# A diffusion backbone on one core: the conditioning projection as row sums on VectorE, GpSimd and ScalarE

## The chip, the cores and the metric

One core of one Trainium2 chip runs the whole kernel in one launch. The metric is the device time of that launch in microseconds (us).

## What is computed

Four layers work on 256 latent tokens and 256 context tokens of width 1024, in fp32. Each layer has a token mixer (neighbourhood attention, retention, convolution, attention again) and a gated feed-forward part (FFN). In front of each stands an RMS norm that is shifted and scaled by the conditioning, and behind each the result is gated by it:

```python
silu_c = jax.nn.silu(c); silu_cc = jax.nn.silu(c_ctx)[None, :]
for i in range(DEPTH):
    mx = jnp.split((silu_c @ ada_w[i] + ada_b[i])[:, None, :], 6, axis=-1)
    mc = jnp.split((silu_cc @ ada_w[i] + ada_b[i])[:, None, :], 6, axis=-1)
    hx = modulate_norm(xs, norm_mix[i], mx[0], mx[1])
    ...
    xs = xs + mx[2] * yx
    hx = modulate_norm(xs, norm_ffn[i], mx[3], mx[4])
    xs = xs + mx[5] * conv_ffn(hx, ffn_w_up[i], ffn_w_dw[i], ffn_b_dw[i], ffn_w_down[i])
```

The conditioning projection is a product of two vectors (one for the context, one for the latent tokens) with four matrices `ada_w[i]` of 1024 by 6144: 6144 features per layer, which are 48 chunks of 128 features. A layer's chunks come in the order shift, scale, gate of the mixer, then shift, scale, gate of the FFN, 8 chunks each.

## The kernel before, in words

Activations lie by feature: 128 features on the partitions, 8 chunks of features, 512 tokens along the row (context, then latent). A dense layer is a row of **tiles**, each 128 output features by 512 tokens in one PSUM bank; a tile takes one **group** of weights (128 x 1024, 512 KB; `_tile_groups`) for 1024 inputs. Every fp32 product is made as three products of a high and a low part (`three`, lines 554 to 556): high by high, low activation by high weight, high activation by low weight. So a group is loaded by SP into `raw` (`refill`, line 402), ScalarE copies it to the high part `Whi` (line 1007), VectorE subtracts for the low part `Wlo` (line 1284, `split`), and TensorE runs 8 x 3 matmuls of 512 columns. There are four slots; the engines split a group three tiles ahead (`LEAD`). SP loads a slot again when TensorE has used it (`weights_used`).

Order of the work in layer 0 behind the first norm: 16 tiles of keys and queries (the mix), 8 groups of values with tokens on the partitions (`tokens_major`), 8 pairs of heads (`pair`, 8 units each: scores on TensorE, bias and maximum on VectorE, exponential on ScalarE, transposes, product with the values), 8 tiles of the output projection (`projected`). Then the second norm (`norm_halves`): the last tiles are made context half first, so that the norm of the context half runs beside the latent half. The FFN is 11 **laps** of 4 tiles (up) and 8 tiles of three groups (down: 8, 8 and 6 blocks of 128, that is 22 x 3 matmuls each). In a lap, VectorE makes three taps of a convolution from tiles 0 and 2 (lines 1702, 1704, 1707), and multiplies tiles 1 and 3 with the GELU (1712) and subtracts for a low part (1716). GpSimd sums the squares for the next norm, one tile behind `residual` (lines 452 and 454: a square and a sum, 512 wide), and in layer 0 stages one head's queries at a time in `Qz` (line 503). In the stages with heads, units wait for each other on three engines.

The conditioning, `mod`, is made from `ada_w` in **slices** of 512 features: 12 per layer, 48 in all. The first four are made ahead of everything (`ada_raw`), the other 44 in places between the tiles: 4 in the mix, 2 in the output projection of layer 0 (`ADA_IN_O`), one in each of the 33 up laps of layers 0 to 2, and 3, 1 and 1 in the down stages (`ada_down`). A slice is loaded by SP (`load_ada`, line 394: four DMAs of 512 KB behind a wait for the slice before), and then made by `ada_slice` (8 products of 32 stationary columns with 512 moving ones, line 653), `ada_rows` on VectorE (line 1295: copy to SBUF), `ada_cols` (4 transposes, line 667), and `ada_store` (lines 1304 and 1306: a small sum, and an add of the bias). TensorE also waits for `mod_ready` ahead of the values (line 739).

Each engine runs its own program in order, and waits on semaphores.

## Time and profile before

| | |
|---|---|
| median of 3 runs | 2718.21 us (2706.47 to 2720.6) |
| the profiled execution | 2714.99 us, of it span 2713.2 us |
| TensorE busy | 96% of the span |
| VectorE, ScalarE, GpSimd busy | 55%, 34%, 10% |
| mean granted TensorE clock | 0.985 |
| DMA | 337.36 MB, mean 124 GB/s |

PE is TensorE's matmuls, PEld its weight loads, DVE VectorE, ACT ScalarE, POOL GpSimd, SP SyncE; a name with a q behind it is the engine's queue. `out<-in` are the program's names, then come partitions x elements. In brackets stands how long the engine sat idle before the instruction, and who ended that.

### The profile page before, as it was taken

How to read it: one execution, taken by the hardware profiler on the slowest of the kernel's cores; microseconds unless marked ns; L12 is line 12 of the kernel's file. 1: busy time of each engine (PE TensorE's matmuls, PEld its weight loads, DVE VectorE, ACT ScalarE, POOL GpSimd, SP SyncE). 2: the span in 40 equal slices, each digit the busy share in tenths (PEclk: the TensorE clock that was granted, in tenths of full speed). 3: DMA queues.
4: the chain of work that ended last, by engine and by line, in shares of the span. 5: the costliest groups of instructions: out<-in, count | busy, mean ns of one | idle time of the engine just before them, and what ended most of it. 6: DMA issues, size and time to landing. Idle time of an engine off the chain costs nothing. (4 is left out here: it accounts for less than half of the span.)

```text
span 2713.2 us, 38419 instructions
## 1 busy us (share of the span) xinstructions
PE 2617.0 (96%) x13796; PEld 2115.7 (78%) x13796; DVE 1482.1 (55%) x2247; ACT 914.3 (34%) x1443; POOL 265.6 (10%) x252
## 2 busy tenths in 40 slices
PE   6999999999999999999999998999999999999999
PEld 3667787777788866788777887878777788778999
DVE  4765645554345344426555338877555436856774
ACT  2225623222232123323222226443222213345543
POOL 5100030000110020030000110003000014102000
PEclk8999999999999999999999999989999999999999
DMA  8531035544423321324444331112545434311455
GB/s 271 166 116 36 0 125 186 178 170 161 156 79 108 111 68 47 124 93 140 178 173 159 125 99 57 55 55 98 177 167 178 155 101 122 109 57 55 157 184 179
DMA packets 94877, 337.36 MB, mean 124 GB/s; under 512 B 11840, under 2 KB 13632, under 8 KB 94656
## 3 DMA queue, kind: packets, MB, share of 16 engines
q1 hardware_dynamic: 90176, 324.28, 34.7%
q0 software_dynamic: 2880, 8.92, 1.5%
q10 hardware_dynamic: 1728, 2.85, 0.3%
q8 instruction: 68, 1.11, 0.2%
q14 instruction: 25, 0.20, 0.0%
HBM read 334.95 MB, written 1.05 MB: 124 GB/s over the span
## 5 line engine op out<-in xcount | busy, mean ns | idle before, releaser
L554 PE MATMUL bank<-Hhi,Whi 128*128 128x512 f32 (+1 forms) x2440 | 883.2, 362 | 37.1 <-DVE Hlo L1340 16.1
L555 PE MATMUL bank<-Hlo,Whi 128*128 128x512 f32 (+1 forms) x2440 | 861.5, 353 | 0.0
L556 PE MATMUL bank<-Hhi,Wlo 128*128 128x512 f32 (+1 forms) x2440 | 860.2, 353 | 0.0
L1284 DVE TENSOR_TENSOR Wlo<-raw,Whi 128x1024 fp32r<-128x1024 f32 x424 | 526.7, 1243 | 387.2 <-ACT Whi L1007 385.4
L1007 ACT ACTIVATE Whi<-raw 128x1024 fp32r<-128x1024 f32 x424 | 447.5, 1057 | 855.9 <-DMA raw<-in_weights 855.4
L554 PEld LDWEIGHTS bank<-Hhi,Whi 128*128 128x128 f32 x2440 | 464.6, 190 | 139.0 <-issue 60.8
L555 PEld LDWEIGHTS bank<-Hlo,Whi 128*128 128x128 f32 x2440 | 465.0, 191 | 63.6 <-issue 4.6
L556 PEld LDWEIGHTS bank<-Hhi,Wlo 128*128 128x128 f32 x2440 | 464.7, 190 | 63.1
L554 PE MATMUL bank<-Ghi,Whi 128*128 128x512 f32 (+1 forms) x770 | 268.6, 349 | 0.0
L556 PE MATMUL bank<-Ghi,Wlo 128*128 128x512 f32 (+1 forms) x770 | 267.1, 347 | 0.0
L555 PE MATMUL bank<-Glo,Whi 128*128 128x512 f32 (+1 forms) x770 | 266.2, 346 | 0.0
L452 POOL TENSOR_TENSOR square<-X 128x512 f32<-128x512 f32 (+1 forms) x58 | 92.0, 1587 | 1517.8 <-DVE X L1399 1509.3
L1702 DVE TENSOR_SCALAR hb<-bank,fff 128x512 f32<-128x512 f32 (+1 forms) x88 | 65.4, 743 | 250.2 <-PE bank L556 248.4
L554 PEld LDWEIGHTS bank<-Ghi,Whi 128*128 128x128 f32 x770 | 144.6, 188 | 22.7 <-DVE X L1399 4.2
L1245 ACT ACTIVATE hb<-hb 128x512 f32<-128x512 f32 (+1 forms) x88 | 51.0, 580 | 327.6 <-DVE hb L1707 327.6
L555 PEld LDWEIGHTS bank<-Glo,Whi 128*128 128x128 f32 x770 | 144.5, 188 | 19.4
L556 PEld LDWEIGHTS bank<-Ghi,Wlo 128*128 128x128 f32 x770 | 144.6, 188 | 18.9
L1399 DVE SCALAR_TENSOR_TENSOR X<-bank,mod,X 128x256 f32<-128x256 f32 x84 | 37.4, 479 | 151.6 <-PE bank L556 151.6
L560 PE MATMUL bank<-Whi,Hhi 128*128 128x512 f32 x256 | 101.8, 398 | 8.0 <-DVE mod L1306 5.4
L1712 DVE TENSOR_TENSOR hb<-hb,bank 128x512 f32<-128x512 f32 (+1 forms) x88 | 54.4, 619 | 86.7 <-PE bank L556 86.7
L561 PE MATMUL bank<-Whi,Hlo 128*128 128x512 f32 x256 | 101.3, 396 | 0.0
L562 PE MATMUL bank<-Wlo,Hhi 128*128 128x512 f32 x256 | 101.0, 395 | 0.0
(194 smaller groups left out, 2879.2 us busy)
## 6 DMA issues: line engine op xcount, KB each, us to landing
raw<-in_weights SPq DMA_DIRECT2D x424, 512.0 KB, 3.3
ada_ring<-in_ada SPq DMA_DIRECT2D x176, 512.0 KB, 5.6
ada_raw<-in_ada SPq DMA_DIRECT2D x16, 512.0 KB, 15.8
rel_in<-in_rpb POOLq DMA_DIRECT2D x48, 128.0 KB, 4.5
decay_t<-in_dist POOLq DMA_DIRECT2D x4, 640.0 KB, 4.2
X<-in_x ACTq DMA_DIRECT2D x1, 2048.0 KB, 10.0
out_y<-X SPq DMA_DIRECT2D x1, 1024.0 KB, 4.8
cos_sin<-in_rope ACTq DMA_DIRECT2D x1, 256.0 KB, 14.2
```

The source lines that it names most:

```text
L452: g.tensor_tensor(square[:, c % 2, tok], X[:, c, tok], X[:, c, tok], ALU.mult).then_inc(sum_step, 1)
L554: t.matmul(dst, Whi[:, st.slot, w], hi, start=start, stop=False)
L555: t.matmul(dst, Whi[:, st.slot, w], lo, start=False, stop=False)
L556: return t.matmul(dst, Wlo[:, st.slot, w], hi, start=False, stop=stop)
L560: t.matmul(dst, hi, Whi[:, st.slot, w], start=start, stop=False)
L561: t.matmul(dst, lo, Whi[:, st.slot, w], start=False, stop=False)
L562: return t.matmul(dst, hi, Wlo[:, st.slot, w], start=False, stop=stop)
L1007: a.activation(Whi[:, st.slot, :], raw[:, st.slot, :], ACT.Copy).then_inc(hi_split, 1)
L1245: a.activation(cv[:, k, tok], cv[:, k, tok], ACT.Gelu_apprx_tanh).then_inc(gelu_done, 1)
L1284: v.tensor_tensor(Wlo[:, st.slot, :], raw[:, st.slot, :], Whi[:, st.slot, :].bitcast(F32), ALU.subtract)\
L1702: v.tensor_scalar(c3, u3, f[:, 0, 1:2], f[:, 0, 3:4], ALU.mult, ALU.add).then_inc(ffn_tap, 1)
L1712: v.tensor_tensor(cv[:, k, tok], cv[:, k, tok], bank[m][:, tok], ALU.mult)\
```

## The change

The first four slices stay. The other 176 chunks of 128 features are no longer made on TensorE. Their weights lie by feature: a chunk is 128 features on the partitions by 1024 inputs, so that one feature's sum runs along a row. At the start TensorE spreads the two conditioning vectors over all partitions (16 products of 128 columns, in the first stage behind slice 1), and ScalarE copies them to `cond`. Then a chunk is loaded by ScalarE's queue into one of three slots of `cond_w`, 512 KB each.

Of a **shared** chunk (115 of them) VectorE makes the latent sum with one scalar_tensor_tensor over 1024 elements that also sums its row (`weigh`), GpSimd then multiplies the slot in place with the context vector (`scale_weights`), ScalarE copies it onto itself and sums the row (`sum_products`), and VectorE adds the bias three chunks later (`cond_store`). Of the other 61 chunks VectorE makes both sums, one after the other. ScalarE loads the slot again when the chunk is summed (`reload`).

Where the chunks go: 8 shared ones beside the values of layer 0, one per group; 8 shared ones beside the pairs of heads, one per pair; 8 not shared in the output projection, two each behind tiles 0 to 2, one each behind 3 and 4; three shared ones in each of the 33 up laps; in the down stages 23 not shared in layer 0 (two each behind groups 0 and 1, one each behind 2 to 20), and 15 in layers 1 and 2 each (groups 0 to 18, but not 3, 7, 11, 15). The loop over pairs of layer 0 is written out on VectorE, ScalarE and GpSimd, as is the first up lap on VectorE. The rope tables are now loaded at the start of the retention instead of at the start of the kernel. The bytes loaded are the same.

```diff
-ADA_SLICES = 6 * D // 512
+MODS = 6 * D // P
 ADA_FIRST = 4
 QUAD = P // 4
-ADA_IN_O = {0: 8, 2: 9}
+COND_SLOTS = 3
+PER_LAP = 3
+IN_V = 8
+IN_HEADS = 8
+IN_O = (0, 0, 1, 1, 2, 2, 3, 4)
+IN_DOWN = ((0, 0, 1, 1) + tuple(range(2, 21)), tuple(g for g in range(20) if g % 4 != 3))
 HALVED = (0, 2, 1, 1, 1, 2, 1, 0)
...
+        p["hosts"] = layer < DEPTH - 1
+        if p["hosts"]:
+            p["cond_up"] = cond + (IN_V + IN_HEADS + len(IN_O) if layer == 0 else 0)
+            p["cond_down"] = p["cond_up"] + PER_LAP * FC // 2
+            cond = p["cond_down"] + len(IN_DOWN[layer > 0])
+            p["cond_end"] = cond
...
+        _, cond_w = region(("cond_skip", [P, 2 * FC * T], F32), ("cond_w", [P, COND_SLOTS, GROUP], F32))
+        _, cond = region(("cond_in_skip", [P, RETENTION], F32), ("cond", [P, 2, D], F32))
+        _, cos_sin = region(("cos_skip", [P, 2 * C * T + 2 * TB * D], F32), ("cos_sin", [P, 2, SEQ], F32))
...
+        def shared(n):
+            return n < IN_V + IN_HEADS or any(p["hosts"] and p["cond_up"] <= n < p["cond_down"] for p in layers)
+        def shared_before(n):
+            return sum(shared(q) for q in range(n))
+        def weighed(n):
+            return 2 * (n + 1) - shared_before(n + 1)
...
-            load_ada(ADA_FIRST)
             for layer, p in enumerate(layers):
-                if layer == 0:
-                    refill(p["mix"], 4, (1,), ADA_FIRST + 1)
-                    refill(p["v"], 2)
-                    refill(p["o"], 1, (0, 2), ADA_FIRST + 5)
-                    refill(p["o"] + SLOTS, 1)
...
+            def scale_weights(n, per=0, i=0):
+                pool.wait_ge(cond_weighed, weighed(n) + per * i)
+                w = cond_w[:, n % COND_SLOTS, :]
+                g.tensor_tensor(w, w, cond[:, 0, :], ALU.mult).then_inc(cond_scaled, 1)
...
+                if layer == 0:
+                    pool.wait_ge(cond_ready, 2)
+                    pool.wait_ge(qz_cleared, 2)
+                    for n in range(IN_V):
+                        scale_weights(n)
...
+                    if layer == 0:
+                        pool.wait_ge(cond_scaled, IN_V + i)
...
+                        pool.wait_ge(q_staged, 2 * i + 2)
+                        scale_weights(IN_V + i)
...
+                if p["hosts"]:
+                    with pool.Fori(0, FC // 2) as i:
+                        for q in range(PER_LAP):
+                            scale_weights(p["cond_up"] + q, PER_LAP, i)
...
-                        if p["ada"] and m == 1:
-                            ada_slice(p["ada"], 1, i)
-                        if p["ada"] and m == 2:
-                            ada_cols(p["ada"] + i)
...
+                if s == 1:
+                    for r in range(2):
+                        for k in range(C):
+                            last = t.matmul(bank[2 * r + k // 4][:, P * (k % 4):P * (k % 4 + 1)],
+                                            csilu[:, k, r:r + 1].to_broadcast([P, P]), ident[:, :],
+                                            start=True, stop=True)
+                        last.then_inc(cond_spread, 1)
...
+            def load_weights(n, per=0, i=0):
+                act.dma_start(cond_w[:, n % COND_SLOTS, :], ada[4 * ADA_FIRST + n + per * i, :, :])\
+                    .then_inc(cond_loaded[n % COND_SLOTS], 16)
+            def sum_products(n, per=0, i=0):
+                nth = shared_before(n)
+                act.wait_ge(cond_scaled, nth + 1 + per * i)
+                w = cond_w[:, n % COND_SLOTS, :]
+                a.activation(w, w, ACT.Copy, accum_out=cond_sum[:, n % COND_SLOTS, 0:1]).then_inc(cond_summed, 1)
+            def reload(n, end, per=0, i=0):
+                if n + COND_SLOTS < end:
+                    if shared(n):
+                        act.wait_ge(cond_summed, shared_before(n) + 1 + per * i)
+                    else:
+                        act.wait_ge(cond_weighed, weighed(n) + per * i)
+                    load_weights(n + COND_SLOTS, per, i)
...
+                        if layer == 0 and s == 5:
+                            sum_products(IN_V + i)
+                            reload(IN_V + i, p["cond_end"])
...
+                act.wait_ge(weights_used, p["mix"])
+                act.dma_start(cos_sin[:, :, :], rope).then_inc(cos_loaded, 16)
...
+                        if p["hosts"] and m >= 2:
+                            for q in ((0,) if m == 2 else (1, 2)):
+                                sum_products(p["cond_up"] + q, PER_LAP, i)
+                                reload(p["cond_up"] + q, p["cond_end"], PER_LAP, i)
...
+                    for n in in_down(layer, m - 1):
+                        reload(n, p["cond_end"])
...
+            for r in range(2):
+                act.wait_ge(cond_spread, r + 1)
+                for k in range(2):
+                    last = a.activation(cond[:, r, 512 * k:512 * (k + 1)], bank[2 * r + k][:, :], ACT.Copy)
+                last.then_inc(cond_ready, 1)
...
+            def weigh(n, spare, per=0, i=0, follows=True):
+                slot = n % COND_SLOTS
+                dve.wait_ge(cond_loaded[slot], 16 * (n // COND_SLOTS + 1) + 16 * (per // COND_SLOTS) * i)
+                if follows:
+                    cond_store(n - COND_SLOTS, per, i)
+                    dve.wait_ge(mod_ready, 4 * ADA_FIRST + n - COND_SLOTS + 1 + per * i)
+                w = cond_w[:, slot, :]
+                first = weighed(n - 1) if n else 0
+                for q, r in enumerate((1,) if shared(n) else (0, 1)):
+                    if first + q:
+                        dve.wait_ge(cond_weighed, first + q + per * i)
+                    last = v.scalar_tensor_tensor(spare[:, :, :].rearrange("p k t -> p (k t)"), w, 1.0, cond[:, r, :],
+                                                  ALU.mult, ALU.mult, accum_out=cond_sum[:, slot, r:r + 1])
+                    last.then_inc(cond_weighed, 1)
+            def cond_store(n, per=0, i=0):
+                slot, k = n % COND_SLOTS, 4 * ADA_FIRST + n
+                earlier = 2 * MODS if k + per >= 2 * MODS else 0
+                dve.wait_ge(cond_weighed, weighed(n) + per * i)
+                if shared(n):
+                    dve.wait_ge(cond_summed, shared_before(n) + 1 + per * i)
+                v.tensor_tensor(mod_slices[:, bass.ds(k - earlier + per * i, 1), :], cond_sum[:, slot:slot + 1, :],
+                                bias_slices[:, bass.ds(k + per * i, 1)].unsqueeze(2).to_broadcast([P, 1, 2]), ALU.add)\
+                    .then_inc(mod_ready, 1)
+            def cond_flush(end):
+                for n in range(end - COND_SLOTS, end):
+                    cond_store(n)
+            def ada_store(index):
...
+                dve.wait_ge(mod_ready, MODS * layer + (6 if part else 3) * C)
                 whole = C - (HALVED[r] if r < 2 * DEPTH else 0)
                 for m in range(whole):
                     st = Step(first + stride * m)
                     for q in range(stride - 1):
                         split(st.ahead(q))
+                        for n in hosted(stride * m + q):
+                            weigh(n, hb)
                     dve.wait_ge(weights_used, st.ahead(stride - 1).n + 1)
                     residual(layer, part, bank[m % 4], m, tok)
                     split(st.ahead(stride - 1))
-                    if m in slices:
-                        ada_rows(slices[m])
-                    if m - 1 in slices:
-                        ada_store(slices[m - 1], earlier)
+                    for n in hosted(stride * m + stride - 1):
+                        weigh(n, hb)
+                if end:
+                    cond_flush(end)
                 if whole < C:
                     for q in range(stride * (C - whole) - 2):
                         split(Step(first + stride * whole + q))
                     norm_halves(r, tuple(range(whole, C)), add_half(layer, part),
                                 [Step(first + stride * C - 2 + n) for n in range(2)])
-            def tokens_major(first, count, dst):
...
+                            if hosts:
+                                weigh(4 * y + quarter, hb, follows=4 * y + quarter >= COND_SLOTS)
...
+                        if layer == 0 and s == 0:
+                            weigh(IN_V + i, hb)
...
+                        if p["hosts"] and m < PER_LAP:
+                            weigh(p["cond_up"] + m, square, PER_LAP, i, not first)
+                projected(layer, 1, p["down"], 3, tok, lambda g: in_down(layer, g))
+                if p["hosts"]:
+                    cond_flush(p["cond_end"])
```

## Rows read from the trace of the kernel before

**Rows 1.** The page, busy time of each engine, share of the span and instructions.
```profile
PE 2617.0 (96%) x13796; PEld 2115.7 (78%) x13796; DVE 1482.1 (55%) x2247; ACT 914.3 (34%) x1443; POOL 265.6 (10%) x252
```

**Rows 2.** The view of waits, TensorE's: engine, line, releaser, us in total, times, longest.
```profile
PE bank L554 <- DVE Wlo L1284: 13.6, 5, 6.2
...
PE bank L667 <- DVE rows L1295: 12.5, 4, 6.4
PE bank L560 <- DVE mod L1306: 5.4, 1, 5.4
```

**Rows 3.** Timeline of TensorE, an up lap of layer 0: start us, us, engine, line, operation.
```profile
470.29 0.39 PE L556 MATMUL bank<-Hhi,Wlo 128*128 128x512 f32 x1
...
475.73 0.39 PE L556 MATMUL bank<-Hhi,Wlo 128*128 128x512 f32 x1
...
480.49 0.39 PE L556 MATMUL bank<-Hhi,Wlo 128*128 128x512 f32 x1
...
482.66 0.50 PE L554 MATMUL bank<-Hhi,Whi 128*128 128x512 f32 x1
...
488.05 0.39 PE L556 MATMUL bank<-Hhi,Wlo 128*128 128x512 f32 x1
...
488.63 0.47 PE L554 MATMUL bank<-Hhi,Whi 128*128 128x512 f32 x1
```

**Rows 4.** Timeline of VectorE: the copy of a slice's rows, in two laps.
```profile
483.25 0.68 DVE L1295 COPY rows<-bank 128x512 f32<-128x512 f32 x1
...
507.60 0.68 DVE L1295 COPY rows<-bank 128x512 f32<-128x512 f32 x1
```

**Rows 5.** Timeline of VectorE: the same lap, tiles 0 and 1.
```profile
475.80 0.81 DVE L1702 TENSOR_SCALAR hb<-bank,fff 128x512 f32<-128x512 f32 x1 [3.34 <-PE bank L556]
...
478.31 1.22 DVE L1284 TENSOR_TENSOR Wlo<-raw,Whi 128x1024 fp32r<-128x1024 f32 x1
480.91 0.69 DVE L1712 TENSOR_TENSOR hb<-hb,bank 128x512 f32<-128x512 f32 x1 [1.38 <-PE bank L556]
481.52 1.22 DVE L1284 TENSOR_TENSOR Wlo<-raw,Whi 128x1024 fp32r<-128x1024 f32 x1
```

**Rows 6.** Timelines of GpSimd and of VectorE near 53 us.
```profile
52.92 6.74 POOL L488 TENSOR_TENSOR rel<-rel_in,mask 128x3072 f32<-128x3072 f32 x1 [8.11 <-DMA rel_in<-in_rpb]
...
53.26 6.69 DVE L1340 SCALAR_TENSOR_TENSOR Hlo<-hb,mod,Hhi 128x256 fp32r<-128x256 f32 x1 [0.19 <-ACT Hhi L1037]
```

**Rows 7.** Timeline of GpSimd near the start: one square, one sum, 512 wide.
```profile
13.32 1.03 POOL L452 TENSOR_TENSOR square<-X 128x512 f32<-128x512 f32 x1
14.44 1.26 POOL L454 TENSOR_TENSOR total<-total,square 128x512 f32<-128x512 f32 x1
```

**Rows 8.** VectorE's groups by form: busy us, mean ns, then idle before.
```profile
L1572 DVE SCALAR_TENSOR_TENSOR hb<-OT,gn,hb 128x512 f32<-128x512 f32 x8 | 6.0, 751 | 26.9 <-ACT hb L1172 26.9
...
L1590 DVE SCALAR_TENSOR_TENSOR Wc<-bank,cvb,odd 128x512 f32<-128x512 f32 x8 | 6.0, 745 | 0.1
```

**Rows 9.** ScalarE's groups by form: the copy of a group, the read of the accumulator.
```profile
L1007 ACT ACTIVATE Whi<-raw 128x1024 fp32r<-128x1024 f32 x424 | 447.5, 1057 | 855.9 <-DMA raw<-in_weights 855.4
...
L1111 ACT ACTIVATION_READ_ACCUMULATOR prob<-bank,peak 128x1 f32 x96 | 19.0, 198 | 0.0
```

**Rows 10.** Timelines near 223 us, VectorE and TensorE, and of a pair of heads.
```profile
223.43 2.48 DVE L1430 COPY V<-bank 128x512 f32<-128x512 f32 x4
...
223.01 1.02 PE L755 MATMUL bank<-QK,Qz 128*128 128x256 f32 x4
...
258.52 0.16 DVE L1485 RECIPROCAL rinv<-psum_p 128x1 f32<-128x1 f32 x1 [0.83 <-PE bank L773]
...
259.57 0.43 DVE L1477 TENSOR_TENSOR bank<-bank,rel 128x256 f32<-128x256 f32 x1 [0.46 <-PE bank L755]
```

**Rows 11.** Timeline of VectorE at the second norm.
```profile
383.21 0.48 DVE L1391 SCALAR_TENSOR_TENSOR X<-bank,mod,X 128x256 f32<-128x256 f32 x1 [2.40 <-PE bank L556]
```

**Rows 12.** Timeline of TensorE in the first stage: four transposes of 128 columns.
```profile
22.18 0.66 PE L667 MATMUL bank<-ident,rows 128*128 128x128 f32 x4
```

More of the change, by code:

```diff
@@ L91, in plan @@
 def plan():
-    group, tile, ready = 0, 0, 0
+    group, tile, ready, cond = 0, 0, 0, 0
     layers = []
@@ L387, in _, with refill @@
                 sp.dma_start(raw[:, s, :], weights[s, :, :]).then_inc(raw_loaded[s], 16)
-            def load_ada(first, per=0, i=0):
-                if not (per == 0 and first == ADA_FIRST):
-                    sp.wait_ge(ada_used, first - ADA_FIRST + per * i)
-                for q in range(4):
-                    sp.dma_start(ada_ring[:, q, :], ada[4 * first + q + 4 * per * i, :, :]).then_inc(ada_loaded[q], 16)
-            def refill(first, laps, ada_after=(), ada_first=0):
+            def refill(first, laps):
                 with sp.Fori(0, laps) as i:
@@ L1238, in ffn @@
                 a.preload_act_table(ACT.Gelu_apprx_tanh)
+                if layer and p["hosts"]:
+                    for n in range(COND_SLOTS):
+                        load_weights(p["cond_up"] + n)
                 for i in bodies(act, FC // 2):
@@ L1400, in residual, with projected @@
                 last.then_inc(tile_free, 1)
-            def projected(layer, part, first, stride, tok, slices, earlier):
+            def projected(layer, part, first, stride, tok, hosted, end=0):
                 r = 2 * layer + 1 + part
+                dve.wait_ge(mod_ready, MODS * layer + (6 if part else 3) * C)
                 whole = C - (HALVED[r] if r < 2 * DEPTH else 0)
@@ L1421, in projected, with tokens_major @@
                                 [Step(first + stride * C - 2 + n) for n in range(2)])
[L1423 removed]
+            def tokens_major(first, count, dst, hosts=False):
                 for i in bodies(dve, count // 2):
@@ L1685, in ffn @@
                 s0 = 1 if last_layer else 0
-                for i in bodies(dve, FC // 2):
+                for i, first in peeled(dve, FC // 2):
                     for m in range(4):
```

140 lines of the change are left out of this document (58 added, 82 removed).

## The prediction

> **What bounds the kernel now.** I read the engines' busy shares first: TensorE is busy in 96% of the span, VectorE in 55%, ScalarE in 34%, GpSimd in 10% [rows 1]. So time on TensorE is worth its full length, if the others can take the work. TensorE's waits came next: little is left in them, and part of it is the conditioning's own: 12.5 us behind the copy of a slice's rows, 5.4 us for `mod` ahead of the values [rows 2]. Then the timeline of one up lap, since 33 of the 44 slices lie in laps. A tile without a slice takes 475.73 - 470.29 = 5.44 us, 24 matmuls at 0.227 us [rows 3]. A lap takes 507.60 - 483.25 = 24.35 us [rows 4]. Four tiles are 21.76 us, so a slice costs TensorE **2.59 us**: one sees 2.17 us between two matmuls where the products stand, 0.58 us where the transposes stand [rows 3], the rest in slower matmuls behind them.
>
> **What is removed.** 44 slices x 2.59 = 114 us of TensorE. Of the 17.9 us of waits I take 10 back: the longest (6.4 us) falls in the first tiles of the mix, where VectorE is late anyway and TensorE would meet the next wait. Saved: 124 us. This is the profiled execution's account (2715.0 us, 3 us below the median shown).
>
> **The price of a chunk.** VectorE: 256 elements take 0.48 us [rows 11], 512 take 0.75 us [rows 8], so 1024 take 1.29 us. Neighbours overlap by 0.09 us (a split is 1.22 us long, 1.13 from start to start), which leaves 1.21. The trace shows no sum along with such an instruction. Its read of the accumulator is bounded by nothing and by ScalarE's 0.20 us [rows 9]; I take 0.15, nearer to the row. With the store (0.15) and a wait on itself (0.12) a shared chunk is 1.63 us, one that VectorE sums twice 3.11 us (another 0.12 between the sums). GpSimd: 512 elements take 1.26 us [rows 7], 3072 take 6.74 us [rows 6], so 1024 take 2.35 us. ScalarE: a copy of 1024 (1.06 us), its read (0.20 us [rows 9]) and the issue of a DMA (0.4), about 1.7 us; at 34% busy this is hidden outside the heads. The 176 loads are the old bytes, moved from SP's queue to ScalarE's; SP's weights no longer queue behind four loads of a slice, which I count as nothing. Its rope load costs VectorE one landing at the start of the retention, 1 us at most on TensorE.
>
> One more price is in the rows: while GpSimd ran its 6.74 us sum, VectorE's instruction with two SBUF operands, 0.48 us elsewhere, took 6.69 us and ended with it [rows 6]. The two exclude each other. `Wlo`, `Glo`, `weigh` and the store have two SBUF operands; the taps and the multiply by a bank have not.
>
> **Up laps.** VectorE: an even tile 478.31 - 475.80 + 1.13 = 3.64, an odd one (481.52 - 480.91) + 1.13 + 0.61 = 2.35 (`Glo` has the width of the multiply) [rows 5]; twice both 12.0, with queue time 12.3 us. Three shared chunks add 4.9. GpSimd's product starts as a chunk's first sum ends. After tile 0 and tile 2 come, on VectorE, a multiply (0.6, no lock) and a split, which waits 1.4 us for GpSimd; after tile 1 come taps, 2.5 us without lock, which cover its 2.35. So 12.3 + 4.9 + 2.9 = **20.1 us in a lap of 21.76**: hidden, with 1.7 us to spare. Splits run three tiles ahead, about 6.5 us early. If that cover went, each microsecond above 21.76 would cost 33.
>
> **Output projection of layer 0.** VectorE per tile: residual 0.8, split 1.14, and GpSimd's square and sum for the norm (1.03 + 1.26 [rows 7]) that now meet a busy VectorE: 4.2 us. Two chunks add 6.2 behind tiles 0 to 2, one adds 3.1 behind 3 and 4: 3 x 10.4 + 2 x 7.3 + 4.2 + 0.5 of stores = 50.5 us, from the end of tile 0 at 5.4 us. VectorE is free for the norm at 56, where today it adds the second context half (as at 383.21 [rows 11]) some 38 us after the stage's start. All of what follows on TensorE hangs on that norm: **+17 us**. Bounds: 10 if GpSimd's work fits into gaps, 22 with loads late.
>
> **Down stages.** Layer 0, a group of 4.99 us (22 x 0.68 / 3): split 1.14, a third of the residual 0.27, chunk 3.11, a third of GpSimd's 2.25: 5.2 with the waits (`weigh` stands in all of 21 groups, twice in two). 21 x 0.25 + 2 x 3.1 = **+12 us** at the norm behind it; bounds 3 and 18. Layers 1 and 2: 15 chunks in 21 groups, 7 x (3.4 + 0.8 + 2.25) + 15 x 3.1 = 92 of 105 us: hidden.
>
> **Values and heads.** The queries of head 0 are now staged in `Qz` behind GpSimd's eighth product, which waits for the last `weigh`: 223.43 (VectorE's last split is done there, the copies of V start [rows 10]) + 1.6 + 2.35 + 0.1 + 0.6 = 228.1, against scores at 223.0 [rows 10]: **+5**. In a pair VectorE gets 1.63 us and ScalarE 1.7 us into a ring without much play; VectorE's idle moments just ahead of the next long unit are 0.83 and 0.46 us [rows 10]. I take 1.2 us per pair, **+10**; bounds 0 and 8 x 3.3 = 27.
>
> **Start.** 16 products of 128 columns behind slice 1; four transposes of that width take 0.66 us [rows 12], so at least 2.6 us, at most three times that in full fp32. Data is waited for there in part: **+3**, bounds 0 and 8.
>
> **Sum.** 2715 - 124 + 17 + 12 + 5 + 10 + 3 + 1 = **2639 us**, 2.9% below the median of before.
>
> **A rule against this change.** With no sum along the row, two fp32 SBUF operands cost nothing: 751 ns with both in SBUF, 745 ns with one in PSUM [rows 8]. The Trainium skill (Vector Engine (DVE) Microarchitecture Reference, Points that are easy to get wrong) says that such a scalar_tensor_tensor with two SBUF sources that are not bf16 runs at half rate, as no port is left for the accumulator. By the rows above this isn't so; none of them has an accumulator, so it is rival 1.
>
> **Rival 1, slower: the summing instruction takes two passes.** Then 1024 elements take 0.2 + 2 x 1.08 = 2.3 us, 1.1 more per sum. A lap becomes 20.1 + 3.3 = 23.4 us on VectorE, above 21.76, which is where it begins to decide: with the slack of the splits spent, about +48 us over 33 laps. The down group of layer 0 becomes 7.4 us (+57), those of layers 1 and 2 overrun by 27 each, the output projection by 17, the heads by 9. Together 185: **2824 us**. For it: no row has the sum. Against it: the equal times of rows 8. 9%.
>
> **Rival 2: no overlap of GpSimd and VectorE at all.** Each product is pushed into VectorE's path, by a lock asked for at the wrong moments or a product in place that is slower than the sum of rows 7: 17.2 + 7.05 = 24.3 us per lap, +2.5 x 33 = 83, of which the lead of the splits takes back some 15. **2707 us**, with a tail above. For it: rows 6. Against it: taps and waits for TensorE leave 9 us of a lap unlocked. 11%.
>
> **Rival 3: the covers hold everywhere.** Heads, norms and start cost 10 instead of 48: **2600 us**. It needs free time on VectorE at the two norms, which the sums deny. 13%.
>
> **Rival 4: the change doesn't relieve TensorE in full,** because loads from ScalarE's queue come late (a reload stands behind a split and a sum) and `weigh`, and every split behind it, waits: each lap has 10 us between a reload and its use, so only the output projection is exposed: 2655 us, inside the forecast.
>
> **How the numbers follow.** Forecast 65% (rival 4 with it), rival 1 9%, rival 2 11%, rival 3 13%, 2% for what I don't see. The forecast's own bounds: all low terms 2639 - 7 - 9 - 10 - 3 - 2 = 2608, all high 2639 + 5 + 6 + 17 + 5 + 8 = 2680. The range 2600 to 2706 takes in rival 3 and the edge of rival 2. A change under 0.5% (13.6 us) can't be told from none here. Faster: forecast, rival 3 and a third of rival 2, 0.82. Same: 0.06. Slower: rival 1, the tail of rival 2, 0.12.
>
> **What would show it.** Right: no products of slices but the first four's; up laps of 21.8 us in all three layers; the scalar_tensor_tensor with a sum at 1.3 us, GpSimd's product at 2.3 to 2.5 us; splits of 2.5 us next to ones of 1.2 us; VectorE's residual rows without idle time in the first two projections, and TensorE waiting for `Hlo` behind both norms of layer 0; VectorE near 1800 us busy. Wrong: laps longer than 22.5 us, or `Wlo` as the main wait of TensorE there; sums above 2 us (rival 1); ScalarE's `prob` late in the heads by far more than 1.2 us per pair.

## The result, and the profile after

The kernel after takes 2620.3 us, median of 4 runs (2613.0 to 2621.1), against 2717.4 us before in the same job. The ratio is **0.965, 95% interval 0.962 to 0.967**: 3.5% faster. The forecast was 2639 us, 2.9% faster, with a range of 2600 to 2706.

The page of the kernel after, busy time of each engine, answers to [rows 1]:

```profile
PE 2521.8 (96%) x12948; PEld 2093.5 (80%) x12948; DVE 1887.9 (72%) x2765; ACT 1044.2 (40%) x1677; POOL 557.3 (21%) x367
```

TensorE has lost 95 us of busy time and is still busy in 96% of the span: what was taken from it shortened the kernel almost one for one. VectorE got 406 us more, GpSimd 292, ScalarE 130. Its waits (engine, line, releaser, us in total, times, longest), against [rows 2]:

```profile
PE bank L575 <- DVE Wlo L1339: 20.2, 11, 6.2
...
PE bank L688 <- POOL total L455: 6.6, 2, 5.9
...
PE bank L762 <- DVE V L1517: 5.9, 2, 4.9
```

The waits for `rows` and `mod` are gone. Those for `Wlo` are not the chunks' doing (19.2 us in experiment 1, which has none). Two stand out in their place, once each: TensorE waits 5.9 us for GpSimd's last sum ahead of the second norm, and 4.9 us ahead of the first scores. The view puts the second down to VectorE's copies of V, but GpSimd stages head 0's queries just as late, and experiment 9 shows that this was the wait that ended last (the scores start at 208.03 us):

```profile
207.32 1.27 POOL L517 COPY Qz<-QK 64x512 f32<-64x512 f32 x2
```

An up lap of layer 0, VectorE's timeline (start us, us, engine, line), against [rows 4, 5]:

```profile
505.14 0.81 DVE L1789 TENSOR_SCALAR hb<-bank,fff 128x512 f32<-128x512 f32 x1 [1.55 <-PE bank L577]
...
508.79 0.15 DVE L1374 TENSOR_TENSOR mod<-cond_sum,bias_ada 128x2 f32 x1
509.07 1.22 DVE L1363 SCALAR_TENSOR_TENSOR square<-cond_w,cond 128x1024 f32<-128x1024 f32 x1
510.22 0.08 DVE L1363 DVE_READ_ACCUMULATOR square<-cond_w,cond 128x1 f32 x1
510.25 0.69 DVE L1799 TENSOR_TENSOR hb<-hb,bank 128x512 f32<-128x512 f32 x1
510.86 3.01 DVE L1339 TENSOR_TENSOR Wlo<-raw,Whi 128x1024 fp32r<-128x1024 f32 x1
...
526.90 0.81 DVE L1789 TENSOR_SCALAR hb<-bank,fff 128x512 f32<-128x512 f32 x1 [1.53 <-PE bank L577]
```

and GpSimd's product in it:

```profile
510.38 2.40 POOL L461 TENSOR_TENSOR cond_w<-cond_w,cond 128x1024 f32<-128x1024 f32 x1 [8.48 <-DVE square L1363]
```

The lap takes 526.90 - 505.14 = **21.76 us**, four tiles of 5.44. VectorE has one idle moment of size in it, 1.55 us, ended by TensorE (the others are of about 0.15 us): it keeps up. A sum of 1024 takes 1.22 us and its accumulator read 0.08. The split that starts at 510.86, while GpSimd multiplies (510.38 to 512.78), takes 3.01 us, not 1.22.

The output projection, VectorE and GpSimd:

```profile
329.93 0.88 DVE L1481 SCALAR_TENSOR_TENSOR X<-bank,mod,X 128x256 f32<-128x256 f32 x2 [6.30 <-PE bank L577]
...
331.85 1.00 DVE L1374 TENSOR_TENSOR mod<-cond_sum,bias_ada 128x2 f32<-128x2 f32 x1
...
334.15 2.20 DVE L1363 SCALAR_TENSOR_TENSOR hb<-cond_w,cond 128x1024 f32<-128x1024 f32 x1
...
338.89 0.87 DVE L1481 SCALAR_TENSOR_TENSOR X<-bank,mod,X 128x256 f32<-128x256 f32 x2
```

```profile
330.88 1.95 POOL L453 TENSOR_TENSOR square<-X 128x512 f32<-128x512 f32 x1 [24.98 <-DVE X L1481]
332.91 2.36 POOL L455 TENSOR_TENSOR total<-total,square 128x512 f32<-128x512 f32 x1
```

A tile with two chunks takes VectorE 8.96 us against TensorE's 5.44. Both sides pay for each other: the square takes 1.95 us and the sum 2.36, against 1.03 and 1.26 alone [rows 7], and on VectorE a store of 0.15 us takes 1.00 and a sum 2.20. The square's 1.95 us aren't the chunks' doing: in experiment 1, which has none, it takes as long beside the split, and the sum 1.29.

### The profile page after: what moved, and what is told of

The parts are those of the page before. It is cut to its first block and busy times, and to the rows that moved or that the text cites. A ratio compares the mean times of both kernels' runs of the same rounds, so it can differ in the third digit from the quotient of the medians.

```text
span 2618.7 us, 37653 instructions
## 1 busy us (share of the span) xinstructions
PE 2521.8 (96%) x12948; PEld 2093.5 (80%) x12948; DVE 1887.9 (72%) x2765; ACT 1044.2 (40%) x1677; POOL 557.3 (21%) x367
## 5 line engine op out<-in xcount | busy, mean ns | idle before, releaser
L1339 DVE TENSOR_TENSOR Wlo<-raw,Whi 128x1024 fp32r<-128x1024 f32 x424 | 638.6, 1508 | 243.1 <-ACT Whi L1009 241.1
L461 POOL TENSOR_TENSOR cond_w<-cond_w,cond 128x1024 f32<-128x1024 f32 x115 | 276.8, 2407 | 559.3 <-DVE square L1363 516.6
L453 POOL TENSOR_TENSOR square<-X 128x512 f32<-128x512 f32 (+1 forms) x58 | 84.8, 1463 | 689.0 <-DVE X L1481 680.1
L1363 DVE SCALAR_TENSOR_TENSOR hb<-cond_w,cond 128x1024 f32<-128x1024 f32 x138 | 185.8, 1346 | 4.7
L577 PEld LDWEIGHTS bank<-Ghi,Wlo 128*128 128x128 f32 x770 | 144.4, 188 | 21.2
L1026 ACT ACTIVATE cond_w<-cond_w 128x1024 f32<-128x1024 f32 x115 | 121.0, 1052 | 36.2 <-POOL cond_w L461 35.6
L1363 DVE SCALAR_TENSOR_TENSOR square<-cond_w,cond 128x1024 f32<-128x1024 f32 x99 | 121.2, 1224 | 11.7
```

The source lines that it names most:

```text
L453: g.tensor_tensor(square[:, c % 2, tok], X[:, c, tok], X[:, c, tok], ALU.mult).then_inc(sum_step, 1)
L461: g.tensor_tensor(w, w, cond[:, 0, :], ALU.mult).then_inc(cond_scaled, 1)
L577: return t.matmul(dst, Wlo[:, st.slot, w], hi, start=False, stop=stop)
L1026: a.activation(w, w, ACT.Copy, accum_out=cond_sum[:, n % COND_SLOTS, 0:1]).then_inc(cond_summed, 1)
L1339: v.tensor_tensor(Wlo[:, st.slot, :], raw[:, st.slot, :], Whi[:, st.slot, :].bitcast(F32), ALU.subtract)\
L1363: last = v.scalar_tensor_tensor(spare[:, :, :].rearrange("p k t -> p (k t)"), w, 1.0, cond[:, r, :], ALU.mult, ALU.mult, accum_out=cond_su ...
```

## The experiments

I compare stages by waypoints in the profiled executions. "Values" is from the first product of V to the first scores, "heads" from there to the first transposes of O, "projection" from the first matmul of the output projection to the reciprocal of the latent half's root in the norm behind it, "FFN" from that reciprocal to the same one a norm later. The stretch ahead of the values, from the first matmul of the mix, is left out: in kernels whose work there is the same it takes from 109.1 us (experiment 11) to 117.6 (experiment 1), with 113.8 in the kernel after, and why isn't known. Such a difference is part of the total times, so the price of a single edit is better read from its stage. Medians are of 4 to 12 runs, those of before of 4 to 17. All times in us:

| kernel | time | ratio to before | values | heads | projection | FFN of layer 0 |
|---|---|---|---|---|---|---|
| before | 2717.4 | 1 | 45.3 | 110.1 | 58.3 | 404.7 |
| before, no slices | 2592.3 | 0.955 (0.951 to 0.958) | 43.9 | 110.0 | 53.2 | 368.2 |
| before, unrolled | 2713.3 | 0.999 (0.998 to 1.001) | 45.2 | 109.0 | 59.9 | 406.5 |
| after | 2620.3 | 0.965 (0.962 to 0.967) | 49.1 | 109.4 | 68.9 | 369.6 |
| after, no chunks | 2600.8 | 0.958 (0.955 to 0.962) | 44.0 | 109.0 | 53.1 | 369.6 |
| after, no squares | 2602.6 | 0.958 (0.956 to 0.960) | 49.1 | 108.6 | 54.8 | 369.6 |

**1. What the new work costs: all chunks left out.** `mod` is 0 behind the first four slices.

```diff
 def weigh(n, spare, per=0, i=0, follows=True):      # also scale_weights, sum_products, load_weights, reload, cond_store
-    ...
+    pass
+dve.wait_ge(mod_ready, 16); dve.sem_inc(mod_ready, 176)
```

> The kernel after, with all 176 chunks left out (loads, sums, products, stores; the entries of mod behind the first four slices are 0 and marked as ready at the start). Theory, from the waypoints of the kernel after: the new work costs about 4 us ahead of the heads, 0 to 1 in them, 10.6 in the output projection, 1 in the first down stage and nothing in laps, some 17 us in all: about 2602 us, the laps 21.76 us as with the chunks, the first projection's end 10 us earlier. Rival: the heads' sums cost what I predicted (10 us) and the unrolled loops of pairs hide it: then the stretch of the heads gets about 10 us shorter and the time is near 2592. Second rival: the loads of the chunks or the busier engines slow the laps or the gate and output stages of the retention: below 2590.

Measured 2600.8 us (2598.9 to 2601.7): all 176 chunks cost **19.5 us** (the three stages below sum to 21.2; the profiled execution's stretch ahead of the values was 3.8 us longer here). The table says where: values 5.1, heads 0.4, projection 15.7, and nothing in the FFN, where 56 of them lie. The row that closes the projection is VectorE's reciprocal, at 392.53 us in the kernel after and here at

```profile
374.25 0.17 DVE L1359 RECIPROCAL token_root<-token_root 128x4 f32<-128x4 f32 x1
```

**2. What the slices cost: before without its 44.** `ada_slice`, `ada_cols`, `ada_rows`, `ada_store` and `load_ada` are taken out behind the first four slices, `mod` is 0 there.

> The kernel before, with its 44 slices behind the first four left out (their loads, products, transposes, copies and stores; mod is 0 there). My account of what is removed was 44 x 2.59 = 114 us of TensorE and 10 us of waits: about 2594 us for a profiled execution at 2715. If a slice's cost in the trace were partly a wait that something else takes over, more than 2605. Rival: every wait for rows and mod goes too, 17.9 us, and the time is 2583.

Measured 2592.3 us (2590.1 to 2596.3), **123.8 below** before's 2716.1 in that job. The 44 x 2.59 us and 10 us of waits hold, to the microsecond and so partly by luck: the interval of the ratio alone is 113 to 133 us, and the profiled executions differ by 118.7. The stage that is least disturbed bears the price of a slice out: the FFN of layer 0 loses 36.5 us with its 14 slices, 2.61 each. The difference of 8.5 us to experiment 1 (3.8 in the profiled executions) is what the rest of the change costs. Of it one sees 0.9 us in the retention, where the rope tables are now loaded, and 1.4 to 1.5 in each FFN of layers 0 to 2. At the start the first reciprocal comes at 35.6 us against 35.0, but in kernels with the same start it comes anywhere from 35.3 to 38.7. The part in the FFNs wasn't foreseen. It shows in all kernels of the new form looked at, with and without chunks, as a step of 0.233 us between matmuls in the down stage of layer 0 (15.40 us per tile) against 0.229 (15.11); which edit causes it stays open.

**3. The lock: up chunks summed twice on VectorE,** so that GpSimd does nothing in the laps.

```diff
 def shared(n):
-    return n < IN_V + IN_HEADS or any(p["hosts"] and p["cond_up"] <= n < p["cond_down"] for p in layers)
+    return n < IN_V + IN_HEADS
```

> The kernel after, with the chunks of the up laps summed twice on VectorE, as those of the down stages are: GpSimd and ScalarE have no part in them. Theory of the lock: VectorE's lap is 12.3 us of its old work and 3 x 2.76 of chunks, 20.6, below 21.76 as with shared chunks (20.2), because the products no longer hold up the splits: every split in a lap 1.22 us long, laps 21.76, the time that of the kernel after within 0.3% (2620). Rival: the splits' 3.01 us have another cause (the weights, the port of PSUM), so they stay, the lap is 12.3 + 2.9 + 8.3 = 23.5 us on VectorE and the time rises by some 50 us to 2670.

Measured 2616.2 us (2615.6 to 2618.3), ratio 0.964 (0.960 to 0.967), the same as after. The split of the same place in the lap, and all splits by VectorE's groups (busy us, mean ns):

```profile
511.93 1.22 DVE L1334 TENSOR_TENSOR Wlo<-raw,Whi 128x1024 fp32r<-128x1024 f32 x1
```

```profile
L1334 DVE TENSOR_TENSOR Wlo<-raw,Whi 128x1024 fp32r<-128x1024 f32 x424 | 533.9, 1261 | 232.7 <-ACT Whi L1005 230.7
```

```profile
L1339 DVE TENSOR_TENSOR Wlo<-raw,Whi 128x1024 fp32r<-128x1024 f32 x424 | 638.6, 1508 | 243.1 <-ACT Whi L1009 241.1
```

The first two are this kernel, the third the kernel after. GpSimd's share of the laps costs VectorE 105 us of blocked splits and saves it 99 sums of 1.27 us, 126 us. VectorE's idle moment in the lap is as long in both kernels, 1.55 and 1.58 us: in the laps, the help of two other engines is worth next to nothing. The Trainium skill (SBUF — State Buffer, Who interferes with whom) says that VectorE and GpSimd share a pair of ports by an exclusive lock, and that the one that issues second is blocked until the first ends; the trace agrees: the split that starts 0.48 us into the product ends 1.09 us behind it, about a full split (1.22 us, 1.13 from start to start) after the product's end.

**4. Where VectorE begins to decide: one more sum per up chunk.**

```diff
+                if per:
+                    v.scalar_tensor_tensor(spare[:, :, :].rearrange("p k t -> p (k t)"), w, 1.0, cond[:, 1, :],
+                                           ALU.mult, ALU.mult, accum_out=extra[:, 0:1]).then_inc(cond_again, 1)
```

> The kernel after, with one more sum of the same form by VectorE for each chunk of the up laps (99 more; it is the price that rival 1 of the prediction had put on a summing instruction, 1.14 us). VectorE has 1.55 us free in a lap and gets 3 x 1.3 = 3.9 us more (with the wait for its accumulator): if VectorE decides from there on, a lap becomes 24.1 us, 2.35 x 33 = 78 us less some 5 per stage for the lead of the splits, so 2620 + 63 to 78 = 2683 to 2698. Rival: part of the sums falls into time in which VectorE would wait for GpSimd's lock anyway, a lap of 22.7 us, 2650.

Measured 2686.3 us (2683.0 to 2689.9), 66 us more than after. TensorE's first wait by size, and two taps of VectorE one lap apart:

```profile
PE bank L577 <- DVE Wlo L1341: 70.5, 85, 6.2
```

```profile
511.46 0.75 DVE L1803 SCALAR_TENSOR_TENSOR hb<-bank,fff,hb 128x510 f32<-128x510 f32 x1 [0.16 <-DVE hb L1800]
...
535.22 0.75 DVE L1803 SCALAR_TENSOR_TENSOR hb<-bank,fff,hb 128x510 f32<-128x510 f32 x1 [0.16 <-DVE hb L1800]
```

A lap is 23.76 us, 2.0 above TensorE's, where 2.35 were expected. So the bound of rival 1 is real: 3.8 us more per lap (3 x 1.27), a little over the 3.3 that two passes per sum would have cost there, takes two thirds of the gain of 97 us away, and by the prediction the down stages would have come on top. That the change pays hangs on the sum running in one pass.

**5. The projection: its chunks without GpSimd's squares.** The norm behind it then sees the last square only.

```diff
+                if r == 1:
+                    pool.sem_inc(sum_step, 2)
+                    return
                 g.tensor_tensor(square[:, c % 2, tok], X[:, c, tok], X[:, c, tok], ALU.mult).then_inc(sum_step, 1)
```

> The kernel after without GpSimd's squares and sums for the second norm (the norm then sees only the last square), which separates the two parts of the 10.6 us that the output projection got longer: the sums themselves, and what GpSimd's locks add to VectorE's instructions there (a second sum of 2.19 us, a store of 1.00 us). Without them VectorE's tile with two chunks should take 8.95 - 1.8 = 7.1 us and one with one chunk less in proportion; the norm comes 7 to 9 us earlier, about 2612. If the locks add nothing and the sums alone fill VectorE, 2618.

Measured 2602.6 us (2599.5 to 2604.2), 10 us further down than expected. VectorE's residual rows of tiles 0 and 1:

```profile
327.28 0.88 DVE L1484 SCALAR_TENSOR_TENSOR X<-bank,mod,X 128x256 f32<-128x256 f32 x2 [7.89 <-PE bank L580]
...
334.42 0.87 DVE L1484 SCALAR_TENSOR_TENSOR X<-bank,mod,X 128x256 f32<-128x256 f32 x2
```

A tile is 7.14 us, as expected, still above 5.44; but the projection is 54.8 us, 14.1 below after and 1.6 above the kernel without chunks. So **14.1 of the 15.7 us come only where the chunks meet GpSimd's squares and sums**, and the eight chunks without them cost 1.6 us or a little more (experiment 1 has the squares, this kernel hasn't). My expectation counted the lock on VectorE's side alone (1.8 us per tile). The 14.1 us have three parts. VectorE's last residual row ahead of the norm starts 48.8 us after the stage's start against 40.4: **8.3 us** of lock. The context half's reciprocal comes 11.4 us later, so **3.1** more: GpSimd is late itself, its last square and sum queue behind those of the tile before and end at 376.04 us, 2.8 after VectorE's residual rows, and TensorE waits 5.9 us for them (up to 0.9 of the 3.1 are already the clock: from its first matmul behind the wait to the reciprocal it takes 2.3 us, in experiment 1 1.4). From that reciprocal to the latent half's it takes 14.2 us against 11.5: **2.7** more, for TensorE's granted clock is at its lower level, 1.2 GHz, behind the wait. Windows (us, busy of each engine, then clock, DMA share, GB/s) of the kernel after and of this one:

```profile
377.00:382.00 5.00, 5.00 (x23) 4.83 (x23) 1.09 (x3) 0.26 (x1) 1.23 (x2) 0.50 0.10 40
```

```profile
361.50:366.50 5.00, 5.00 (x43) 4.95 (x42) 2.90 (x8) 1.17 (x3) 0.00 (x0) 1.00 0.32 107
```

TensorE makes 23 matmuls in 5 us there instead of 43.

**6. Squares on ScalarE,** for the first six tiles of X; the sums stay on GpSimd, and nothing is left out.

```diff
+                def square_early(c):
+                    act.wait_ge(tile_free, FREE0 + p["mix_tile"] + 24 + 1 + c)
+                    act.wait_ge(sum_step, sum_first(1) + 1 + 2 * max(0, c - 1))
+                    a.activation(square[:, c % 2, :], X[:, c, :], ACT.Square).then_inc(squared, 1)
```

> The kernel after, with the squares of the first six chunks of X for the second norm made by ScalarE (busy 28% of that stage) and only their sums left to GpSimd. In the run without GpSimd's squares and sums the output projection and the norm took 14.1 us less (54.8 against 68.9 us from the first matmul of the stage to the image's reciprocal), but that kernel left work out. Theory: GpSimd's two instructions per tile and VectorE's exclude each other, and what is late in the end is GpSimd's last total: with one of the two gone, 7 to 12 of the 14.1 us come back, 2609 to 2613. Rival: the sums (1.26 us) are the half that hurts, or ScalarE's squares put its splits back: under 4 us, 2617 or more.

Measured 2614.9 us (2612.1 to 2615.7), ratio 0.962 (0.960 to 0.964): 5.5 us better, and the projection 63.3 us, 5.5 less. Less than expected, more than the rival said. Of the 5.5 us, 0.8 are the clock: TensorE still waits 4.6 us and still falls to the lower level (0.50), but comes back sooner. A tile takes VectorE 8.1 us, since the sum alone still blocks a `weigh`, and is blocked itself, 2.24 us for 1.26:

```profile
350.50 2.24 POOL L456 TENSOR_TENSOR total<-total,square 128x512 f32<-128x512 f32 x1 [5.86 <-ACT square L1175]
```

**7. The projection's chunks in the heads,** as shared ones, two per pair (`IN_HEADS = 16`, `IN_O = ()`, `weigh` at units 0 and 4).

> The kernel after, with the 8 chunks of the output projection of layer 0 moved into the heads as shared chunks (two per pair, at units 0 and 4). Theory: the output projection gets its old length back (-10.6 us at the norm behind it, VectorE done with the residuals before TensorE's last tiles), and the heads have room for a second sum of 1.3 us on VectorE and of 1.7 us on ScalarE in a pair of 13.16 us (VectorE 75% busy there, ScalarE 74%): 0 to 3 us more, so 2620 - 9 = 2611. Rival: each sum in the ring costs about 1.2 us, as I had predicted for the first: +10 in the heads, 2620.

Measured 2609.4 us (2606.3 to 2611.2), ratio 0.961 (0.959 to 0.962): 11 us better than after. The projection is back at 53.2 us; the heads take 114.9 us, 5.5 more. The first sum of a pair was nearly free (0.4 us for eight), the second costs 0.7 us each.

**8. Was the heads' cost hidden by the unrolled loops?**

```diff
-                with dve.Fori(1, C) as i:
-                    pair(i, False)
+                for i in range(1, C):
+                    pair(i, False)
```

The same for ScalarE and GpSimd, layer 0 only.

> The kernel before, with the loops over the pairs of layer 0 unrolled on GpSimd, ScalarE and VectorE as the change has them. If the unrolled loops hide a cost of the heads' sums, the heads get about 10 us shorter here, 2708. If they do nothing and the sums stand in idle time, the time is that of before, 2717, and the stretch of the heads about as long as before (110.1 us from the first scores to the first transposes).

Measured 2713.3 us, ratio 0.999 (0.998 to 1.001). The heads take 109.0 us against 110.1: the unrolling gives 1.1 us, no more. The sums stand in idle time, which the kernel after shows too. A sum in a pair, and TensorE in the same microseconds, with no idle time noted in front of any of its rows:

```profile
222.74 1.23 DVE L1363 SCALAR_TENSOR_TENSOR hb<-cond_w,cond 128x1024 f32<-128x1024 f32 x1
```

```profile
222.44 0.60 PE L770 MATMUL bank<-ident,prob 128*128 128x128 f32 x4
222.88 1.00 PE L780 MATMUL bank<-V,probT 128*128 x8
223.72 1.08 PE L762 MATMUL bank<-QK,Qz 128*128 x2
```

**9. Head 0's queries ahead of the products.**

```diff
+                    for par in range(2):
+                        half = slice(64 * par, 64 * par + 64)
+                        g.tensor_copy(Qz[half, par, tok], QK[half, 0, tok]).then_inc(q_staged, 1)
-                    for n in range(IN_V):
+                    for n in range(IN_V + 1):
                         scale_weights(n)
```

> The kernel after, with GpSimd staging the queries of head 0 ahead of its nine products for the chunks of the values, not behind them. TensorE waits 4.95 us ahead of the first scores with the chunks; the copies of Qz end 0.6 us after GpSimd's product. Theory: the staging is what the scores wait for, the wait falls to about 1 us and the kernel gains 3 to 4 us, all of it ahead of the scores: 2616. Rival: the scores wait for VectorE's copies of V, which the last sum has put back, and nothing or under 1 us is gained.

Measured 2622.9 us (2615.7 to 2625.6), ratio 0.964 (0.963 to 0.966): nothing gained. The first scores do start 5.1 us earlier after the first product of V (44.0 against 49.1), but the heads take 116.4 us instead of 109.4. TensorE's timeline there:

```profile
207.76 2.08 PE L766 MATMUL bank<-QK,Qz 128*128 128x512 f32 x2 [4.52 <-DVE V L1521]
211.22 0.69 PE L774 MATMUL bank<-ident,prob 128*128 128x128 f32 x2 [1.39 <-ACT prob L1142]
```

The wait has moved behind the first four scores: VectorE copies V behind its eighth sum, and ScalarE, whose own queue holds the eighth chunk's sum, makes the first exponential behind it and behind a table load of 1.28 us.

**10 and 11. The eighth sum of the values moved into the first pair** on VectorE and ScalarE (10), and with the squares on ScalarE as well (11). The queries stay ahead of the products, as in experiment 9.

```diff
-                            if hosts:
+                            if hosts and (y, quarter) != (1, 3):
                                 weigh(4 * y + quarter, hb, follows=4 * y + quarter >= COND_SLOTS)
...
-                        if layer == 0 and s == 0:
+                        if layer == 0 and s == (4 if i == 0 else 0):
                             weigh(IN_V + i, hb)
+                        if layer == 0 and i == 0 and s == 1:
+                            weigh(IN_V - 1, hb)
```

> The kernel after, with head 0's queries staged ahead of the products (as before), and with the eighth sum of the values moved behind VectorE's copies of V into the first pair, on ScalarE too. Staging the queries first moved the first scores 5.1 us earlier but only put the wait of 4.5 us behind the second score, where it was V's copies and, on ScalarE, the eighth sum. If these were what was left, the transposes of O come 4 to 5 us earlier than in the kernel after (153.5 to 154.5 us after the first product of V instead of 158.5): 2616. Rival: the first pair has no room for two sums, what is gained ahead of it is lost in it: 2620.

> Both edits of the two runs beside it in one kernel. They lie in different stages, so the gains add up if each is real: 11 to 16 us below the kernel after, 2604 to 2609, and at or below the kernel with all eight chunks of the output projection moved into the heads (2609.4). If the second falls, 2609 to 2613.

Measured 2619.2 us (2616.6 to 2623.6; ratio 0.964, 0.962 to 0.966) and 2609.6 us (2605.1 to 2614.7; 0.961, 0.959 to 0.963). In 10, values and heads together take 156.1 us against 158.5: 2.4 us of the 4 to 5 expected, too small to be told in the median. The two sums in the first pair cost 2.7 us there. In 11 the stages give 2.3 and 6.6 us, together 8.9, a little over the 2.4 and 5.5 of the two edits alone. The median gives 10.7; the stretch ahead of the values, which the edits don't touch, was 4.7 us shorter in the profiled execution.

**12. Four chunks in the projection, four more in the heads,** with the later eighth sum and GpSimd's squares as they were.

```diff
-IN_HEADS = 8
-IN_O = (0, 0, 1, 1, 2, 2, 3, 4)
+IN_HEADS = 12
+IN_O = (0, 1, 2, 3)
+HOSTS = dict(zip((1, 4, 8, 12, 16, 24, 28, 32, 40, 44, 48, 56, 60), range(7, 20)))
```

`HOSTS` gives the unit, counted over the pairs, of each sum that VectorE makes in the heads.

> The kernel with the later eighth sum of the values, and the 8 chunks of the output projection divided: 4 more into the heads (every second pair gets two), 4 left in tiles 0 to 3 of the output projection, one each, GpSimd's squares unchanged. From the runs: 8 chunks more in the heads cost 5.5 us there, so 4 cost 2 to 3; a tile of the output projection with one chunk takes VectorE about 0.8 + 1.2 + 2.6 + 1 to 2 us of locks = 5.6 to 6.6 us against TensorE's 5.44, four of them put it back by at most 4.5 us, and tiles 4 and 5, without a chunk, take that back: stage and norm 53 to 57 us, against 68.9 in the kernel after and 53.2 without chunks; the tail of the values gives 1 to 2.5. Sum: 2620 - 14 + 3 - 2 = 2607, 2604 to 2611; at best 5 us below the kernel with all eight in the heads. Rival: the pairs with two sums cost as much as all of them did (5.5 us), and the locks cost the norm 4 us: 2612.

Measured **2603.9 us** (2601.2 to 2608.9), ratio **0.960 (0.958 to 0.962)**. It is the fastest kernel here that computes everything, 16 us below after (its slowest run lies below after's fastest, 2613.0) and 3 above the kernel with no chunks at all. By stages the gain is 14.0 us and the distance to no chunks 7.3: values 44.0 us, heads 115.4, projection 54.0. The stretch ahead of the values took 109.2 us, near the low end of what it takes, and flatters the total. A tile with one chunk takes VectorE 6.34 us, and the two tiles without one take the arrears back, so that TensorE's wait for the total falls from 5.94 us to 0.52. Its granted clock stays at 1.00 behind that wait, and from one half's reciprocal to the other's it takes 11.5 us, as without chunks:

```profile
324.85 0.88 DVE L1496 SCALAR_TENSOR_TENSOR X<-bank,mod,X 128x256 f32<-128x256 f32 x2 [5.92 <-PE bank L591]
...
331.19 0.87 DVE L1496 SCALAR_TENSOR_TENSOR X<-bank,mod,X 128x256 f32<-128x256 f32 x2
```

```profile
360.00 0.61 PE L702 MATMUL bank<-one,total 128*128 128x2 f32 x4 [0.52 <-POOL total L456]
```

## Why the prediction was right, and where its sizes were not

**The saving held.** 124 us predicted, 123.8 measured (experiment 2).

**The costs were too high**, 48 us: 44 for the chunks against 19.5, and 4 for the start and the rope tables against 4 to 8.5 for all the rest, most of it elsewhere. The median came 19 us below the forecast for that reason, inside the range:

- *Down stage of layer 0, +12: nothing.* The step that failed is above all the price of a chunk summed twice, 3.11 us. I had a sum at 1.21, its read at 0.15 and a wait of 0.12 behind each. The read takes 0.08 us, overlaps what follows, and only one 0.12 stands between the two sums: 657.55 to 660.15, 2.60 us with the store. TensorE's side was a little off too: a tile takes it 15.40 us in this stage (VectorE's residual rows, when they wait for TensorE, come at 722.34 and 737.74), not three times 4.99. Over a tile of three groups VectorE takes 663.89 - 650.07 = 13.82 us:

```profile
650.07 0.87 DVE L1481 SCALAR_TENSOR_TENSOR X<-bank,mod,X 128x256 f32<-128x256 f32 x2
...
657.55 0.15 DVE L1374 TENSOR_TENSOR mod<-cond_sum,bias_ada 128x2 f32<-128x2 f32 x1
657.73 1.22 DVE L1363 SCALAR_TENSOR_TENSOR hb<-cond_w,cond 128x1024 f32<-128x1024 f32 x1
...
660.15 1.22 DVE L1339 TENSOR_TENSOR Wlo<-raw,Whi 128x1024 fp32r<-128x1024 f32 x1
663.89 0.87 DVE L1481 SCALAR_TENSOR_TENSOR X<-bank,mod,X 128x256 f32<-128x256 f32 x2
```

  So a group of 5.2 us against 4.99 had made a cost where one of 4.6 against 5.13 makes none: next to a bound, half a microsecond decides over the sign of the margin, and 21 groups multiply it. The sign that the prediction named, residual rows without idle time, holds in the output projection, but here for the first four tiles only, while VectorE makes up for the doubled groups; from the fifth on it idles 1.1 to 1.5 us in front of them.
- *Heads, +10 at 1.2 us per pair: 0.4 us for all eight* (109.4 against 109.0; the unrolling gives 1.1 us back besides). I took the idle moments just ahead of a long unit for the ring's play [rows 10]. Experiment 7 shows that play: one sum fits, a second costs 0.7 us.
- *Projection, +17: 15.7.* The size was right by luck; the mechanism was half of it. I let VectorE's 50.5 us decide, with 3.11 for a chunk and 2.3 per tile for GpSimd's square and sum. It took 43.4 us (329.93 to the end of its residual rows at 373.29; 2.60 for a chunk, and 1.8 of lock in a tile, 8.96 - 7.14), so that VectorE alone is 10 us late where I had 17. The missing 5 are two things that weren't in the sum: GpSimd's total comes later than VectorE's last row, and TensorE's clock is at its lower level behind the wait for it (experiment 5).
- *Queries of head 0, +5: 5.1.* The row named, the staging behind GpSimd's eighth product, was right as the first thing late, but experiment 9 shows V's copies and ScalarE's sum right behind it: taking it away gave nothing.
- *Start, +3: not told from none.* The 16 products take 3.7 us on TensorE (2.6 to 7.8 were the bounds), but the first reciprocal moves by 0.6 us between experiments 1 and 2, less than it varies. *Rope tables, +1: 0.9.* Unforeseen: 1.4 to 1.5 us in each of three FFNs.

**Up laps: right in mechanism and sum.** 20.1 us of VectorE in a lap of 21.76, with 1.7 us to spare: measured 1.55 idle, and no loss. GpSimd's product takes 2.40 us against 2.35. The two blocked splits of a lap cost 1.8 and 1.6 us where I had 1.4 each, a chunk 1.5 where I had 1.63; the two errors cancel. VectorE's total was named as near 1800 us and is 1888.

**The rivals.** Rival 1, two passes per sum, is refuted by 1.22 us for 1024 elements, the same as a split. The Trainium skill's rule (Vector Engine (DVE) Microarchitecture Reference, Points that are easy to get wrong), that such an instruction with two SBUF sources that aren't bf16 runs at half rate for want of a port to read the accumulator back, doesn't hold for it here. Rival 1's price for the laps, 48 us for 3.3 us more on VectorE, agrees with the 66 us that 3.8 us more cost in experiment 4. Rival 2, no overlap, is refuted by the laps, though its lock is confirmed by experiment 3. Rival 3, all covers hold (2600), is nearly what the FFNs and heads did; only the values and the projection kept it from coming true, and experiment 12 comes near it (2603.9) by moving five chunks' sums into the heads and thinning out the projection's. Rival 4, late loads, wasn't tried by itself; a chunk lands 3.8 us (median) after its issue, and the lap shows no wait for one.

## What to carry to other kernels

Work moved off a bound engine is paid in whole where the helpers have idle time per period, and in laps that could be read from the old timeline to 0.2 us. The costs sit at the seams: put no side work where another engine's small jobs feed a norm that everything waits for, and spread it thinly enough that a few free tiles take the arrears back. An engine that shares a lock with the busy one may take from it nearly what it gives. And a wait on TensorE can cost more than its length: the one of 5.9 us here cost 2.7 us more in slower matmuls behind it.

## What the hardware showed that I had not expected

- A store of 128 x 2 elements on VectorE, 0.15 us alone, took 1.00 us beside GpSimd's square: the lock's price goes by the other engine's instruction, not by one's own. It goes both ways: GpSimd's sum took 2.36 us instead of 1.26 beside VectorE's sums, and its square 1.95 instead of 1.03 beside the split, with or without chunks.
- VectorE's accumulator read (0.08 us) is far cheaper than ScalarE's (0.20 us [rows 9]) and costs next to nothing from start to start.
- In the gate and output stages of the retention TensorE's granted clock fell to its lower level, 1.2 GHz, for some microseconds around a wait of 3.6 us for `Ylo`, in the kernel after and in others. It isn't a cost of the chunks: the kernel before without its slices has a fall as deep as any, and its retention takes 2.5 us more than that of the kernel before, whose profiled execution had none. Nor is it tied to the slices: the unrolled kernel before, with all its slices, has a fall too (0.66 over 5 us), and its retention is no longer than before's. Windows (us, busy of each engine, then clock, DMA share, GB/s) of before, of before without slices and of before unrolled:

```profile
1137.30:1142.30 5.00, 3.72 (x16) 3.08 (x17) 2.45 (x3) 2.37 (x3) 0.00 (x0) 1.00 0.97 342
```

```profile
1077.57:1082.57 5.00, 3.75 (x9) 2.98 (x10) 2.41 (x3) 2.34 (x2) 0.00 (x0) 0.50 0.12 46
```

```profile
1129.17:1134.17 5.00, 5.00 (x16) 3.94 (x15) 1.22 (x1) 0.81 (x1) 0.00 (x0) 0.66 0.85 321
```

  What decides whether it falls there isn't known.
